# A two-layer mixer kernel on one core: ScalarE's and VectorE's order around the first attention head, the GELU and the output product

## What is computed

```python
x = layer_norm(ALPHA * x + 0.5 * swiglu_ffn(x, ffn1_w_up[l], ffn1_w_down[l]), ln1_g[l], ln1_b[l])
mix = hybrid_mixer(x, w_in[l], ..., w_glu, w_branch[l], w_out[l], rel_bias)
x = layer_norm(ALPHA * x + mix, ln2_g[l], ln2_b[l])
x = layer_norm(ALPHA * x + 0.5 * swiglu_ffn(x, ffn2_w_up[l], ffn2_w_down[l]), ln3_g[l], ln3_b[l])
```

```python
u, q, k, v, qi, ki, wi, g_ssm, g_attn = jnp.split(x @ w_in, splits, axis=-1)
# branch A: complex diagonal state-space scan over time, then
y = jax.nn.gelu(y); y_ssm = y * jax.nn.sigmoid(y @ w_glu)
# branch B: an indexer (relu scores, weighted sum over 8 heads) picks 64 keys per query,
# softmax attention over them with a relative bias, 8 heads
merged = jax.nn.sigmoid(g_ssm) * (y_ssm @ w_branch[0]) + jax.nn.sigmoid(g_attn) * (y_attn @ w_branch[1])
return merged @ w_out
```

## Time and profile before

| | |
|---|---|
| median of three runs | 1171.94 us (1167.6 to 1172.6) |
| the profiled execution | 1174.14 us |
| its span in the profile | 1172.2 us |
| mean granted TensorE clock | 0.993 of full speed |
| TensorE matmuls busy | 1147.5 us (98% of the span) |
| VectorE, ScalarE, GpSimd busy | 763.9, 556.7, 405.8 us |
| read from HBM | 205.56 MB, 176 GB/s over the span |

### The profile page before, as it was taken

How to read it: one execution, slowest core, us unless ns; L and a number is a source line. 1 busy time by engine, 2 the same in 40 slices (tenths; PEclk the granted TensorE clock), 3 DMA queues, 4 the chain that set the end, 5 groups by cost and what they waited for, 6 DMA issues and landing times.

```text
span 1172.2 us, 17704 instructions
## 1 busy us (share of the span) xinstructions
PE 1147.5 (98%) x5932; PEld 934.0 (80%) x5932; DVE 763.9 (65%) x1086; ACT 556.7 (47%) x795; POOL 405.8 (35%) x567
## 2 busy tenths in 40 slices
PE   8999999999999999999999999999999999999997
PEld 6888878877777788888788888887877778888885
DVE  5657746789747865675486555477896478645544
ACT  5545433574554454454245445336745535544430
POOL 2889885117600278997700000010374001000001
PEclk9999999999999999999999999999999999999999
DMA  8766653743526576666357575535454365757540
GB/s 261 229 210 196 216 175 106 224 131 112 174 73 216 177 207 204 186 218 211 117 175 231 169 245 187 191 93 187 157 165 127 121 204 164 226 185 232 189 152 36
DMA packets 158720, 207.50 MB, mean 177 GB/s; under 512 B 13145, under 2 KB 107673, under 8 KB 158657
## 3 DMA queue, kind: packets, MB, share of 16 engines
q1 hardware_dynamic: 154928, 201.70, 54.1%
q10 hardware_dynamic: 2704, 3.36, 1.0%
q0 software_dynamic: 1024, 1.61, 0.8%
HBM read 205.56 MB, written 1.06 MB: 176 GB/s over the span
## 4 chain that ended last, share of the span: by engine, by line
PE 82%; DVE 7%; ACT 4%; issue 3%; DMA 3%; SPq 0%; POOLq 0%; POOL 0%; DVEq 0%; ACTq 0%
PE ps L700 25%; PE ps L702 25%; PE ps L701 25%; DVE wlo L1130 4%; PE ps L727 2%; DMA raw<-in_w_in 1%; DVE score L1287 1%; PE ps L942 1%; ACT whi L400 1%; DMA raw<-in_ffn_w_up 1%; PE ps L717 1%; PE ps L894 1%; PE ps L963 1%; DMA raw<-in_w_branch 1%; PE ps L953 0%
## 5 line engine op out<-in xcount | busy, mean ns | idle before, releaser
L1130 DVE TENSOR_TENSOR wlo<-raw,whi 128x1024 fp32r<-128x1024 f32 (+1 forms) x372 | 484.1, 1319 | 193.3 <-ACT whi L400 179.8
L400 ACT CAST whi<-raw 128x1024 fp32r<-128x1024 f32 (+1 forms) x372 | 385.4, 1044 | 290.8 <-PE ps L702 231.0
L700 PE MATMUL ps<-whi,xh 128*128 128x512 f32 (+1 forms) x1056 | 420.9, 399 | 4.9 <-DVE wlo L1130 4.4
L702 PE MATMUL ps<-whi,xl 128*128 128x512 f32 (+1 forms) x1056 | 411.7, 390 | 0.0
L701 PE MATMUL ps<-wlo,xh 128*128 128x512 f32 (+1 forms) x1056 | 411.0, 389 | 0.0
L700 PEld LDWEIGHTS ps<-whi,xh 128*128 128x128 f32 x1056 | 199.8, 189 | 50.3 <-DVE wlo L1130 9.9
L702 PEld LDWEIGHTS ps<-whi,xl 128*128 128x128 f32 x1056 | 199.6, 189 | 41.9
L701 PEld LDWEIGHTS ps<-wlo,xh 128*128 128x128 f32 x1056 | 199.8, 189 | 37.5
L1492 POOL TENSOR_TENSOR rstd<-var_eps,cst 128x1 f32<-128x1 f32 x12 | 18.2, 1517 | 562.3 <-DVE var_eps L1177 562.3
L700 PE MATMUL ps<-whi,hh 128*128 128x512 f32 x352 | 141.3, 401 | 0.0
L702 PE MATMUL ps<-whi,hl 128*128 128x512 f32 x352 | 138.9, 395 | 0.0
(11 more groups left out here) (185 smaller groups left out, 1110.5 us busy)
## 6 DMA issues: line engine op xcount, KB each, us to landing
raw<-in_ffn_w_up SPq DMA_DIRECT2D x352, 256.0 KB, 4.0
raw<-in_ffn_w_down SPq DMA_DIRECT2D x176, 256.0 KB, 3.0
raw<-in_w_in SPq DMA_DIRECT2D x128, 256.0 KB, 3.4
raw<-in_w_branch SPq DMA_DIRECT2D x32, 256.0 KB, 3.0
raw<-in_w_out SPq DMA_DIRECT2D x32, 256.0 KB, 4.7
bias_g<-bias_rows ACTq DMA_DIRECT2D x16, 192.0 KB, 3.8
raw<-in_w_in SPq DMA_DIRECT2D x16, 148.0 KB, 2.3
affine<-in_ln_g SPq DMA_DIRECT2D x4, 512.0 KB, 5.2
```

What stands on the lines that cost most here:

```text
L400: nc.scalar.copy(whi[:, s % RING, 0:w], raw[:, s % RAW, 0:w]).then_inc(S["hi_done"], 1)
L700: nc.tensor.matmul(o, ah, bh, start=start, stop=False)
L702: return nc.tensor.matmul(o, al, bh, start=False, stop=stop)
L1130: nc.vector.tensor_tensor(wlo[:, s % RING, 0:w], raw[:, s % RAW, 0:w], f32(whi[:, s % RING, 0:w]), ALU.subtract).then_inc(S["split_done"], 1)
```

## The change

Nothing is computed otherwise. On TensorE the first two index scores come one quarter later. On ScalarE: the transposed u is copied ahead of a split and the second index read follows one split, not two; a one-column activation (`load_table`) in ScalarE's program ahead of the tanh of gate group 5 calls for the exponentials' table, and one behind head 7's exponentials for the GELU's; only s+20 and s+21 are split ahead of head 0, s+22 and s+23 at j = 1 and 2; the GELU moves from j = 15 to j = 16. On VectorE: the turn of state quarter 2 moves from ahead of head 0's logits to j = 1, its scan from j = 1 to j = 3; the splits of s+20 to s+28 are spread otherwise over j = 3 to 13. In the output product all four splits of the last group come ahead of the second merged half, on both engines.

```diff
@@ -73,7 +73,7 @@
 
 PAIR_IN = [(2, 0, 0), (2, 0, 3)]
 TURN_AT = [(1, 1, 1), (2, 0, 1), (3, 1, 3), (4, 0, 2)]
-IDX_AT = [(2, 1, 0), (2, 1, 2), (3, 0, 2)]
+IDX_AT = [(2, 1, 1), (2, 1, 3), (3, 0, 2)]
 OUT_AT = [(5, 1, 1), (6, 0, 1), (6, 1, 3), (7, 1, 1)]
 ATT_C = 6
 LAST_K = 3
@@ -587,15 +587,19 @@
                 nc.scalar.copy(ya_h[:, :, tok(t)], ps[:, TB - t, :].rearrange("p (k n) -> p k n", k=4)
                                ).then_inc(S["yah_done"], 1)
 
+            def load_table(func):
+
+                nc.scalar.activation(started[:, 2:3], started[:, 0:1], func)
+
             def mixer(l):
                 s = mix(l, MIX0 + RING)
                 splits(s)
                 proj_read(l, 0, 1)
                 proj_read(l, 1, 0)
-                splits(s + 4, 2)
                 pt_read(l, 0)
+                splits(s + 4, 1)
                 proj_read(l, 1, 1)
-                splits(s + 6, 2)
+                splits(s + 5, 3)
                 bu_copy(l, 0)
                 pt_read(l, 1)
                 bu_copy(l, 1)
@@ -616,8 +620,9 @@
                 proj_read(l, 4, 0)
                 splits(s + 16)
                 proj_read(l, 4, 1)
+                load_table(ACT.Exp)
                 proj_read(l, 5, 0)
-                splits(s + 20)
+                splits(s + 20, 2)
                 proj_read(l, 5, 1)
 
                 def gelu(g):
@@ -635,15 +640,19 @@
                             prt_read(l, r - 1)
                         if r < N_HEADS:
                             exp_probs(l, r)
+                            if r == N_HEADS - 1:
+                                load_table(ACT.Gelu_apprx_tanh)
                         if 2 <= r:
                             att_out(l, r - 2)
+                    if 1 <= j < 3:
+                        splits(s + 21 + j, 1)
                     if 4 <= j < 8:
                         splits(s + 20 + j, 1)
                     if 12 <= j < 16:
                         splits(s + 16 + j, 1)
                     if j % 4 == 3:
                         proj_read(l, ATT_C + j // 8, j // 4 % 2)
-                    if j == 15:
+                    if j == 16:
                         gelu(0)
                         gelu(1)
                 for g in range(2):
@@ -671,9 +680,8 @@
                     nc.scalar.mul(xh[:, :, tok(t)], src, 0.5).then_inc(S["mh_done"], 1)
 
                 m_hi(0)
-                splits(mix(l, BRA0 + RING), 3)
+                splits(mix(l, BRA0 + RING))
                 m_hi(1)
-                splits(mix(l, BRA0 + RING + 3), 1)
                 transition(3 * l + 2, mix(l, FFN2_0))
 
 
@@ -1332,7 +1340,6 @@
                 select(l, 0)
                 select(l, 1)
                 splits(s + 16)
-                ssm_turn(l, 2)
 
                 def gate_merge(t):
                     if t == 0:
@@ -1352,21 +1359,21 @@
                         if 1 <= r < N_HEADS + 1:
                             invert(l, r - 1)
                     if j == 1:
+                        ssm_turn(l, 2)
+                    if j == 3:
                         ssm_scan(l, 2)
                         splits(s + 20, 1)
-                    if j == 3:
-                        splits(s + 21, 3)
                     if j == 5:
                         ssm_turn(l, 3)
                     if j == 7:
                         ssm_scan(l, 3)
-                        splits(s + 24, 1)
+                        splits(s + 21, 1)
                     if j == 9:
-                        splits(s + 25, 2)
+                        splits(s + 22, 2)
                     if j == 11:
-                        splits(s + 27, 1)
+                        splits(s + 24, 3)
                     if j == 13:
-                        splits(s + 28, 1)
+                        splits(s + 27, 2)
                         dve.wait_ge(S["y_used"], NQ * (l + 1))
                         dve.wait_ge(S["d_landed"], 16 * (l + 1))
                         for q in range(NQ):
```

## The result

The changed kernel takes 1184.51 us (median of four runs, 1183.95 to 1185.77), the kernel before 1169.87 in the same comparison (the three runs on record and a fourth of 1167.8 us). The ratio is 1.0126, interval 1.0096 to 1.0155: 1.26% slower. The forecast was 1177.3 within 1169 to 1187. The profiled execution took 1184.75 us with a span of 1182.6, against 1174.14 and 1172.2 before: 10.6 us more by the two profiles, 14.6 by the medians.

A forecast was written before the change was run, and what follows sets the result against it. TensorE was taken as the bound, busy 1147.5 of 1172.2 us. Losses 4.5 + 5.4 + 0.8 less gains 3.8 + 1.5 gave +5.4: 1179.5 from the profile, 1177.3 forecast against the runs' median, range 1169 to 1187.

The forecast's parts named there:

- The prediction's own case: Whole kernel: new waits in the attention rounds outweigh the gains, +5.4 us, range 1172 to 1183; chance 0.78.
- rival 3: Attention rounds: longer waits from 5.45 us transfers, the scan's upper end and longer lower clock; 10.6 us more, 1188; chance 0.10.
- the sum: Whole kernel: 4.5 and 5.4 us lost in the layers' attention rounds, 0.8 for scans, less 3.8 and 1.5: +5.4.
- the first head: Head 0's exponentials: earlier table load and fewer splits ahead remove TensorE's wait, 1.97 + 1.7 and 1.1 + 1.7 us.
- the GELU: Attention rounds: moving it removes 1.71 us wait and 1.75 us lower-clock loss per layer; 0.4 charged at the GLU product.
- the beginning: Mixer's beginning: later split of s+5 and later index scores remove waits of 2.7 and 1.1 us, 3.8 in all.
- the output product: Output product: fourth split ahead of the second merged half removes 0.77 us of wait twice, 1.5 in all.
- The walk: Layer one's attention rounds, step by step: TensorE +1.2 us at head 3, +5.9 at head 4, +7.6 with lower clock.
- turn with logits 5.96: VectorE, layer one, before s+21's low split: the state turn together with a head's logits takes 5.96 us.
- the scan 0 to 0.8, I take 0.4: VectorE's scan 3 beside GpSimd's turn back: 0 to 0.8 us extra per layer, middle value 0.4 taken.
- Lower clock after it, 1.7: TensorE after the wait ahead of head 4: work lost at the lower clock, 1.7 us, making +5.9 into +7.6.
- The 6.9 us that the sum counts for this: Attention rounds, both layers: lower-clock loss after the first-head and GELU waits, expected back within the 18.7 us gain.

The follow-up runs named there:

- the early taker alone: The changed kernel with VectorE's loop order of before, ScalarE's and all other edits kept: 1158.6 us, ratio 0.9895 to the kernel before.
- the late release alone: The changed kernel with ScalarE's high splits of s+25 to s+27 moved behind the exponentials, VectorE's order kept: 1166.65 us, ratio 0.9965 to the kernel before.

## Why the prediction was right, and where its sizes were off

**The sign was right and the size was not.** +5.4 us were forecast; the medians give +14.6, the two profiles +10.6. The prediction's own case had 1172 to 1183, and 1184.5 lies above it. The time is inside the stated 1169 to 1187 only because that range was stretched towards rival 3, whose main term did not come (see below). That much of it is luck.

**The place and the mechanism** were right. ScalarE waited for s+25 in one piece (12.11 us; "some 10" was said), then for s+26 and s+27 (4.73 + 1.07); the wait for the states was 3.35 and 3.44 us (3.1 said) and did not add to the path; the transfers took 3.4 us from low split to high split (3.5 taken). Undoing either end of the chain removed TensorE's waits for probabilities.

**The parts that were to gain** came as in the sum. By TensorE's places in the two traces, both layers together: the first head 6.7 us (6.5 predicted), the GELU 5.8 (6.1), the beginning 4.0 (3.8), the output product 2.1 (1.5), 18.6 against 17.9 in all. The table load cost its 1.28 us and no drain: it stands at 337.42, and head 5's output follows at 338.82. By "ScalarE: Activation LUTs", What ACT_TABLE_LOAD costs, of the Trainium skill, some 1.38 us more would lie between them; the one-column activation that does stand between takes 0.20.

**The new waits** were taken too small. From head 2 to head 5 TensorE loses 13.8 and 14.8 us. The walk had 11.3 in each layer (in layer one the 3.7 gained and the 7.6 lost), and the sum 0.4 more each for the scan. The terms that were mis-sized:

- *"turn with logits 5.96"*. The row was taken where GpSimd's products ended at 301.66, in the middle of the turn (298.97 to 304.09): its last two parts took 0.69 us each. With scan 2 moved back, GpSimd starts later as well, and its work now covers the whole turn: 6.8 us instead of 5.1, with logits 8.0. The walk moved VectorE's instructions and kept a duration that depended on where the neighbour's work lay.
- *"the scan 0 to 0.8, I take 0.4"*. It is 3.25 against 2.32, so 0.9, and 1.1 in layer two (3.40): beyond the upper bound that was set, though GpSimd's products ended at 303.93 and lay beside only part of it. The bound was low because it took 1.6 us for a split beside GpSimd. The trace of before also has three splits that lie wholly beside GpSimd's products, and they take 2.1 us each:

```profile
292.04 6.35 DVE L1130 TENSOR_TENSOR wlo<-raw,whi 128x1024 fp32r<-128x1024 f32 x3
```

The Trainium skill's rule in "GPSIMD Engine Reference", Specifications, names this contention for instructions with two SBUF inputs and gives no size. By it the upper end would hold, which was the better guide. The turn's 2.0 and the scan's 0.9 us, less some 0.7 for steps that were shorter than taken (the split of s+21 took 1.19, not 1.6), put head 3 at 311.9 where the walk, less the 1.45 us from the beginning, has 309.7.

- *"Lower clock after it, 1.7"*. From head 4 to head 5 the excess over a round of 5.18 us is 6.95 - 5.18 = 1.8 us in layer one, but 2.95 in layer two, where the wait ahead of it was 4.36 us.
- *The median.* The three terms above make the 5.2 us between the forecast's 1179.5 and the profiled 1184.75; that the gains came 0.7 larger is nearly made up by 0.4 us lost ahead of the first mixer, where the first wait for a low split took 2.25 us instead of 1.46. The remaining 2.0 us up to the median's miss of 7.2 are the step from profile to median: the profiled execution of before lay 2.2 above its runs, and this was carried over to the kernel after, which lies 0.2 above its own.

**Why the two profiles differ by 10.6 and the medians by 14.6.** Of 25 runs of the kernel before in one group, the fastest took 1166.81 us at a mean granted clock of 0.999, the slowest 1174.46 at 0.993. The profiled execution of before stands at 0.993: all four waits of TensorE in its attention rounds were followed by the lower clock. The 6.9 us that the sum counts for this are only partly in the median. The changed kernel ran at 0.984 to 0.990 each time. Rival 3 had the size nearly right (1188), and of its terms the smaller ones: the scan beyond its upper end, and more clock lost after a long wait. Its main term, 3.9 of 4.3 us per layer for slower transfers, did not come: the transfers took what the forecast took. The slower turn stood in for it.

## What to carry to other kernels

Where a split frees a buffer, follow the freed buffer through the request and the transfer to the *other* engine's next split, and look at what stands behind that one in program order. Here neither the early taker alone (1158.6 us) nor the late release alone (1166.65 us, with the states' wait left) made TensorE wait for the probabilities, and both together cost some 18 us more than the latter, 1.5%. Take the duration of an instruction that is slower beside another engine's work for the overlap that it will have, not the one it had. And before a gain at the lower clock is put into a sum, see in several runs how often the clock falls there.

## What the runs showed of the hardware

- **The clock after a wait.** The same wait is followed by the lower clock in one layer and not in the other. With the beginning and output edits alone, the wait of 1.71 us behind the GELU stands in both layers (TensorE goes on at 335.24 and 906.58). The stretch behind it has 0.66 in layer one, and in layer two 905 to 910 and 910 to 915 both have 1.00:

```profile
335.00:340.00 5.00, 4.76 (x22) 4.32 (x23) 1.16 (x2) 1.21 (x4) 0.00 (x0) 0.66 0.34 105
...
910.00:915.00 5.00, 5.00 (x45) 5.00 (x44) 0.69 (x1) 0.60 (x1) 0.00 (x0) 1.00 0.14 47
```

In the run with ScalarE's splits later, TensorE waited 3.35 us for the states in layer one and 3.44 in layer two, and the clock fell after the second alone:

```profile
305.00:310.00 5.00, 5.00 (x41) 3.61 (x30) 2.59 (x9) 1.28 (x6) 4.84 (x4) 1.00 0.38 108
...
875.00:880.00 5.00, 4.96 (x42) 3.59 (x42) 2.19 (x2) 0.00 (x0) 3.77 (x3) 0.66 0.31 108
```

What decides it is not settled here. The waits of 1.2 and 1.5 us in the mixer's beginning were followed by no fall in the profiled execution of before.

- **VectorE beside GpSimd.** A 128x512 sum on VectorE takes 0.69 us alone and 1.55 to 1.77 beside GpSimd's products, the 128x1024 product with the table 1.22 and 2.20, two scans 2.32 and 3.25 to 3.40, a split 1.20 and 2.1 (6.35 us for three). Not every instruction is slowed alike: the turn's first 128x1024 product took 1.28 us in layer one of the change and 1.58 in layer two, both beside GpSimd. GpSimd's own product of 128x512 takes between 1.2 and 2.3 us. VectorE's part of that is shown by leaving GpSimd's work out; GpSimd's part was only seen, not tried.
